# Inputs and result in the chip's own layouts; square root on ScalarE, its inverse on VectorE

## What is computed

```python
def layer_norm(x, g, b):
    mu = jnp.mean(xf, -1, keepdims=True)
    var = jnp.mean(jnp.square(xf - mu), -1, keepdims=True)
    return (xf - mu) * lax.rsqrt(var + LN_EPS) * g + b

def first_block(x, mem, ...):
    for i in range(DEPTH):                      # 2 layers
        h = diff_attention(x, ...) if i % 3 == 0 else dilated_attention(x, ...)
        x = layer_norm(ALPHA * x + h, ...)
        x = layer_norm(ALPHA * x + memory_cross_attention(x, mem, ...), ...)
        x = layer_norm(ALPHA * x + conv_glu(x, ...), ...)
    return x

def second_block(x, ...):
    proj = rms_norm_2(x, g_mix) @ w_in
    ...                                         # gated linear attention, sparse attention
    x = x + mixed @ w_out
    return x + hier_moe(rms_norm_2(x, g_ffn), ...)   # 32 experts
```

## Time and profile before

| | |
|---|---|
| median of 3 runs | 3189.44 us |
| lowest, highest | 3189.18, 3193.69 us |
| the profiled execution | 3190.67 us |
| its span, first to last instruction | 3188.9 us |
| TensorE: matmul, weight loads | 3019.6 us, 2417.7 us busy |
| VectorE, ScalarE, GpSimd | 1220.5, 1177.4, 1186.4 us busy |
| TensorE's mean granted clock | 0.96 |

### The profile page before, as it was taken

One profiled execution on the slowest core, in us unless ns is written; L12 is line 12 of the kernel. 1 busy time (PEld: TensorE's weight loads), 2 busy tenths in 40 slices (PEclk: granted clock), 3 DMA queues, 4 the chain that ended last, 5 costly groups with the idle time before them and its releaser, 6 DMA issues.

```text
span 3188.9 us, 38472 instructions
## 1 busy us (share of the span) xinstructions
PE 3019.6 (95%) x15009; PEld 2417.7 (76%) x15009; DVE 1220.5 (38%) x2249; ACT 1177.4 (37%) x1564; POOL 1186.4 (37%) x514
## 2 busy tenths in 40 slices
PE   8998998999989999998898999979989998999999
PEld 6765866888878888886866888858856876888887
DVE  2556327442432332335417443349143034232222
ACT  3565434322343343433434322363452234222222
POOL 3221523444433322231523444433232443444443
PEclk9999999999999999999999999988966999999999
DMA  4202412333342222211321333222211233343442
GB/s 136 67 27 67 132 53 66 94 104 93 108 124 80 67 72 75 67 54 61 124 67 53 104 94 92 85 64 70 76 35 48 77 101 89 117 119 99 122 112 83
DMA packets 366624, 269.30 MB, mean 84 GB/s; under 512 B 13328, under 2 KB 358851, under 8 KB 366476
## 3 DMA queue, kind: packets, MB, share of 16 engines
q1 hardware_dynamic: 366412, 267.14, 28.0%
q10 hardware_dynamic: 64, 0.10, 0.0%
HBM read 265.01 MB, written 6.39 MB: 85 GB/s over the span
## 4 chain that ended last, share of the span: by engine, by line
issue 46%; PE 35%; POOL 17%; ACT 1%; DVE 1%; POOLq 0%; DMA 0%; ACTq 0%; DVEq 0%; SPq 0%
POOL wl L592 11%; PE ps L1760 10%; PE ps L1761 10%; PE ps L1762 10%; POOL wl L590 6%; PE ps L2170 1%; PE ps L2187 1%; PE ps L1756 1%; PE ps L2091 0%; PE ps L2136 0%; PE ps L2159 0%; DVE X L1367 0%; POOLq L597 0%; PE ps L2074 0%; ACT X L826 0%
## 5 line engine op out<-in xcount | busy, mean ns | idle before, releaser
L590 POOL TENSOR_TENSOR wl<-raw,wh 128x1024 fp32r<-128x1024 f32 (+1 forms) x239 | 563.3, 2357 | 1902.8 <-ACT wh L632 1902.8
L1760 PE MATMUL ps<-xh,wh 128*128 128x512 f32 x2192 | 874.0, 399 | 48.5 <-issue 34.8
L1761 PE MATMUL ps<-xh,wl 128*128 128x512 f32 x2192 | 860.4, 392 | 0.0
L1762 PE MATMUL ps<-xl,wh 128*128 128x512 f32 x2192 | 859.7, 392 | 0.0
L632 ACT ACTIVATE wh<-raw 128x2048 fp32r<-128x2048 f32 (+1 forms) x239 | 450.6, 1886 | 901.6 <-PE ps L1762 859.2
L592 POOL TENSOR_TENSOR wl<-raw,wh 128x1024 fp32r<-128x1024 f32 (+1 forms) x239 | 605.8, 2535 | 0.0
L1760 PEld LDWEIGHTS ps<-xh,wh 128*128 128x128 f32 x2192 | 415.4, 190 | 164.3 <-issue 68.7
L1762 PEld LDWEIGHTS ps<-xl,wh 128*128 128x128 f32 x2192 | 415.4, 189 | 88.9
L1761 PEld LDWEIGHTS ps<-xh,wl 128*128 128x128 f32 x2192 | 415.9, 190 | 82.5
L1760 PE MATMUL ps<-ah,wh 128*128 128x512 f32 x864 | 340.0, 393 | 4.8 <-DVE X L1367 2.9
L1762 PE MATMUL ps<-al,wh 128*128 128x512 f32 x864 | 336.4, 389 | 0.0
(11 more groups left out here) (324 smaller groups left out, 3416.6 us busy)
## 6 DMA issues: line engine op xcount, KB each, us to landing
raw<-in_ffn_w_in SPq DMA_DIRECT2D x88, 512.0 KB, 5.0
raw<-in_dil_w_qkv SPq DMA_DIRECT2D x72, 512.0 KB, 4.6
raw<-in_w_in SPq DMA_DIRECT2D x42, 512.0 KB, 4.5
raw<-in_xatt_w_kv SPq DMA_DIRECT2D x32, 512.0 KB, 4.0
raw<-in_ffn_w_out SPq DMA_DIRECT2D x32, 512.0 KB, 4.1
raw<-in_w_gate SPq DMA_DIRECT2D x32, 512.0 KB, 5.0
raw<-in_w_up SPq DMA_DIRECT2D x32, 512.0 KB, 6.1
raw<-in_w_down SPq DMA_DIRECT2D x32, 512.0 KB, 4.5
```

What stands on the lines that cost most here:

```text
L590: pool.tensor_tensor(wl[:, s, 0:4, 0:n], raw[:, s, 0:4, 0:n], wh[:, s, 0:4, 0:n].bitcast(F32), ALU.subtract)
L1760: pe.matmul(dst, stat_h, mov_h, start=first, stop=False)
L1761: pe.matmul(dst, stat_l, mov_h, start=False, stop=False)
L1762: return pe.matmul(dst, stat_h, mov_l, start=False, stop=last)
```

## The change

- The host hands over `x` and `mem` already in the layout of `X`, and the parameters as the finished tile `par`; it turns the result back. So the transposes of x, of the parameters, of `mem` and of the result go, with their copies out of PSUM.
- SyncE loads unit 0, then x in four transfers, then unit 1, and the rest behind. ScalarE runs `high(0)` behind the second `xh`. The bias matmuls stand behind unit 2, and ScalarE's wait for the bias line's transfer stands at the fifth item of the attention.
- `mh` and `ml` are formed from the tile `memory_in` in SBUF, not from PSUM.
- The result leaves `X` directly, two chunks a transfer, each when its unit's additions are done.
- In the norms ScalarE takes a square root into `rstd`, and VectorE its reciprocal into bank `RSTD`. `roots()` loads ScalarE's table for the square root ahead of the units whose result a norm takes in (seven places in the program's run).

```diff
@@ sync
+            qkv = a["diff_w_qkv"][0]
+            square(Lin(0), qkv, 0)
+            for n in range(4):
+                sp.dma_start(X[:, 2 * n:2 * n + 2, :], a["x"][:, 2 * n:2 * n + 2, :]).then_inc(x_in[n], 16)
+            square(Lin(1), qkv, D)
             sp.dma_start(lamb[:, :, :].rearrange("p a b -> p (a b)"),
...
-            for role in range(2):
-                square(Lin(role), qkv, role * D)
...
+            sp.dma_start(par[:], a["params"]).then_inc(p_in, 16)
+            sp.dma_start(const[:], a["const"].rearrange("p (n m) -> p n m", m=P)).then_inc(const_in, 16)
...
-                sp.dma_start(mrows[:], a["mem"][0].rearrange("(t p) d -> p t d", p=P)).then_inc(m_in, 16)
+                sp.dma_start(memory_in[:], a["mem"]).then_inc(m_in, 16)
...
-            orows = out[0].rearrange("(t p) d -> p t d", p=P)
-            for q in range(4):
-                sp.wait_ge(o_cp, 2 * q + 2)
-                sp.dma_start(orows[:, :, q * UC:(q + 1) * UC], orow[:, :, q * UC:(q + 1) * UC]).then_inc(o_out, 16)
+            for k in range(4):
+                u = UNITS - 4 + k
+                sp.wait_ge(drained[u % 2], u // 2 * 2 + 2)
+                sp.dma_start(out[:, 2 * k:2 * k + 2, :], X[:, 2 * k:2 * k + 2, :]).then_inc(o_out, 16)
@@ scalar
+            def roots():
+                act.preload_act_table_set("sqrt_and_others")
+
+            for c in range(KC):
+                act.wait_ge(x_in[c // 2], 16)
+                act.activation(xh[:, c], X[:, c], ACT.Copy).then_inc(xh_ready, 1)
+                if c == 1:
+                    high(Lin(0))
+            high(Lin(1))
             act.wait_ge(lam_d, 4)
             act.activation(lam_e, lam_s, ACT.Exp).then_inc(lam_x, 1)
...
-            act.wait_ge(zs_out, 16)
+            def bias_line():
+                act.wait_ge(z_mm, 2)
+                for j in range(2):
+                    act.activation(zline[:, j * T:(j + 1) * T], ps[0:8, 5 + j], ACT.Copy).then_inc(z_cp, 1)
+                act.wait_ge(z_cp, 2)
+                act.dma_start(zscratch, zline[:]).then_inc(zs_out, 16)
...
+            bias_line()
             for n in range(DIFF_ITEMS + 6):
+                if n == TT:
+                    act.wait_ge(zs_out, 16)
                 diff_step(n)
...
                     act.wait_ge(ln_dve, 2 * n + 2)
-                    act.activation(rstd[:], acc_s[:, 0], ACT.Ln).then_inc(ln_act, 1)
+                    act.activation(rstd[:], acc_s[:, 0], ACT.Sqrt).then_inc(ln_act, 1)
...
-                    act.activation(rstd[:], ps[:, SQUARE], ACT.Ln, bias=eps_rms).then_inc(ln_act, 1)
-                act.wait_ge(ln_act, on_act - 1)
-                act.activation(ps[:, RSTD], rstd[:], ACT.Exp, scale=-0.5).then_inc(ln_act, 1)
+                    act.activation(rstd[:], ps[:, SQUARE], ACT.Sqrt, bias=eps_rms).then_inc(ln_act, 1)
...
             def memory(layer):
                 for b in range(4):
-                    act.wait_ge(mt_done, 4 * layer + b + 1)
-                    act.activation(mh[:, 2 * b:2 * b + 2, :], ps[:, 4 + b].rearrange("p (k t) -> p k t", k=2), ACT.Copy
+                    act.wait_ge(m_in, 16 * layer + 16)
+                    act.activation(mh[:, 2 * b:2 * b + 2, :], memory_in[:, 2 * b:2 * b + 2, :], ACT.Copy
                                    ).then_inc(mh_done, 1)
...
             def after_attention(layer):
+                roots()
...
+                roots()
                 residual(U_MO[layer], n0 + 1)
...
+                        roots()
                         residual(u0 + width, n0 + 2)
...
+            roots()
             residual(U_OUT, 7)
@@ vector
+            for c in range(KC):
+                dve.wait_ge(xh_ready, c + 1)
+                dve.tensor_tensor(xl[:, c], X[:, c], xh[:, c].bitcast(F32), ALU.subtract).then_inc(xl_ready, 1)
             dve.wait_ge(lam_in, 16)
...
                     for c in range(4):
                         centre(c)
                 dve.wait_ge(ln_act, on_act)
+                dve.reciprocal(ps[:, RSTD], rstd[:]).then_inc(inverse, 1)
+                own(inverse, n + 1)
...
-                    dve.tensor_tensor(ml[:, 2 * b:2 * b + 2, :], ps[:, 4 + b].rearrange("p (k t) -> p k t", k=2),
+                    dve.tensor_tensor(ml[:, 2 * b:2 * b + 2, :], memory_in[:, 2 * b:2 * b + 2, :],
                                       mh[:, 2 * b:2 * b + 2, :].bitcast(F32), ALU.subtract).then_inc(ml_done, 1)
@@ tensor
...
                 columns(Lin(0), xh, xl, ready=ready)
                 columns(Lin(1), xh, xl)
                 rows(Lin(2), xh, xl)
+                pe.wait_ge(z_in, 32)
+                for j in range(2):
+                    pe.matmul(ps[0:8, 5 + j, :], relb[:], hot[:, j * T:(j + 1) * T], start=True, stop=True
+                              ).then_inc(z_mm, 1)
+                pe.wait_ge(z_cp, 2)
+                pe.wait_ge(const_in, 16)
                 for n in range(DIFF_ITEMS + 4):
                     diff_step(n)
```

More of the change, by code:

```diff
@@ L270, in program @@
         drained = [sem("drained0"), sem("drained1")]
-        x_in, p_in, m_in, lam_in, z_in, zs_out = (sem(n) for n in ("x_in", "p_in", "m_in", "lam_in", "z_in", "zs_out"))
+        x_in = [sem(f"x_in{n}") for n in range(4)]
+        const_in, p_in, m_in, lam_in, z_in, zs_out = (
+            sem(n) for n in ("const_in", "p_in", "m_in", "lam_in", "z_in", "zs_out"))
         zc_out, mean_mm, keep_mm = sem("zc_out"), sem("mean_mm"), sem("keep_mm")
-        xt_done, par_t, par_s = sem("xt_done"), sem("par_t"), sem("par_s")
+        par_s = sem("par_s")
         z_mm, z_cp = sem("z_mm"), sem("z_cp")
@@ L279, in program @@
         stat_mm, ln_act, ln_dve = sem("stat_mm"), sem("ln_act"), sem("ln_dve")
-        cent, nrm, z_ready = sem("cent"), sem("nrm"), sem("z_ready")
+        cent, nrm, z_ready, inverse = sem("cent"), sem("nrm"), sem("z_ready"), sem("inverse")
         dbias_in = sem("dbias_in")
@@ L308, in program @@
         m_y, m_hh, m_hl = sem("m_y"), sem("m_hh"), sem("m_hl")
-        o_tr, o_cp, o_out = sem("o_tr"), sem("o_cp"), sem("o_out")
+        o_out = sem("o_out")
         f_cd, f_left, f_gd, f_hh, f_hl = (sem("f_" + n) for n in ("c", "left", "g", "hh", "hl"))
-        NORM_AT = [(n + 1, 3 * n + 3) for n in range(6)] + [(6, 20), (8, 22)]
+        NORM_AT = [(n + 1, 2 * n + 2) for n in range(6)] + [(6, 13), (8, 14)]
         MEAN, SQUARE, VAR, RSTD = 4, 5, 6, 7
@@ L650, in copy_out @@
                 copy_half(u, 1, dst, func, scale)
+            def roots():
[6 more added lines that the diff above has]
+            high(Lin(1))
             act.wait_ge(lam_d, 4)
             act.activation(lam_e, lam_s, ACT.Exp).then_inc(lam_x, 1)
[L655 to L663, removed]
-            act.activation(subln8, par[:, 0, R_SUBLN:R_SUBLN + 1], ACT.Copy, scale=1 - LAMBDA_INIT).then_inc(par_s, 1)
[L665 to L669, removed]
-            act.wait_ge(zs_out, 16)
+            act.wait_ge(p_in, 16)
+            act.activation(subln8, par[:, 0, R_SUBLN:R_SUBLN + 1], ACT.Copy, scale=1 - LAMBDA_INIT).then_inc(par_s, 1)
+            def bias_line():
[4 more added lines that the diff above has]
+                act.dma_start(zscratch, zline[:]).then_inc(zs_out, 16)
             def diff_store(u, role, j):
@@ L798, in norm @@
             def norm(n, g_row, b_row=None, keep=False, memory=None):
-                event, on_act = NORM_AT[n]
+                event, _ = NORM_AT[n]
                 if b_row is not None:
@@ L1190, in _ @@
                 over(act, u0 + PART_EXPERTS, 4, skip)
-            for c in range(KC):
-                act.wait_ge(o_tr, c + 1)
-                act.activation(orow[:, :, c * P:(c + 1) * P], ps[:, 4 + c % 4].rearrange("p (t n) -> p t n", t=TT),
-                               ACT.Copy).then_inc(o_cp, 1)
         @block.vector
@@ L1224, in _ @@
             dve.tensor_scalar(neglam, neglam, LAMBDA_INIT, None, ALU.subtract).then_inc(lam_d, 1)
-            for c in range(KC):
-                dve.wait_ge(xh_ready, c + 1)
-                dve.tensor_tensor(xl[:, c], ps[:, c % 4], xh[:, c].bitcast(F32), ALU.subtract).then_inc(xl_ready, 1)
             own(lam_d, 6)
@@ L1997, in after_attention @@
                 columns(Lin(u0 + 1), ah, al)
-                pe.wait_ge(m_in, 16 * (layer + 1))
-                for b in range(4):
-                    for k in range(2):
-                        for t in range(2):
-                            tr = flip(ps[:, 4 + b, k * M + t * P:k * M + (t + 1) * P],
-                                              mrows[:, t, (2 * b + k) * P:(2 * b + k + 1) * P])
-                    tr.then_inc(mt_done, 1)
                 columns(Lin(u0 + 2), ah, al)
@@ L2251, with by_chunk, parameters @@
         "w_out_2", "g_ffn_2", "w_rg_2", "b_rg_2", "w_re_2", "b_re_2", "w_gate_2", "w_up_2", "w_down_2"]
+def by_chunk(rows):
+    return np.ascontiguousarray(rows.reshape(rows.shape[0], KC, P).transpose(2, 1, 0))
+def parameters(inputs):
+    par = np.zeros((P, 3, P), np.float32)
```

(17 more changed lines are left out.)

58 lines of the change are left out of this document (6 added, 52 removed).

## The result

The changed kernel takes 3201.4 us in the median of six executions (3198.6 to 3206.1), against 3191.1 for the kernel before in six beside it. The ratio is 1.0033, with a 95% interval of 1.0020 to 1.0046. Measured again on another chip, both unchanged, it is 1.0033 (1.0022 to 1.0045). So it is slower, by about 10 us; the forecast of 3191 missed by that, though its range held the time. The profiled execution took 3198.6 us with a span of 3196.8, 7.9 more than before.

The account below looks back on a forecast made before the run. TensorE, busy 95% of the span, was taken as the bound. Terms -9.5 + 3.1 + 0.9 + 13.2 - 6.0 gave +1.7 us on the 3188.9 span, so 3191.0 us forecast, range 3177 to 3205.

Parts of the forecast that it names:

- The likeliest case: Whole kernel: time stays within the 0.2%, 6.4 us, that a measurement can tell; chance 0.53.
- the slow rival: Reciprocal takes 4.6 us on VectorE in all eight norms, TensorE waiting: total +12.9, 3202 us; chance 0.18.
- R: Time of one 128x512 reciprocal on VectorE in each norm; forecast 3.2 us, between ends of 0.69 and 4.6.
- The 178 ns row: Narrow reciprocal in the router, in the trace before; read as 8.7 ns an element, giving the 4.6 us upper end.
- The rule for norms 1, 2, 4 and 5: In these norms the first product starts R - 0.26 us later, the reciprocal standing behind four centrings.
- The sum of the norms: All eight norms together: 8R - 12.4, forecast as +13.2 us.
- R - 3.15: Claimed change in each of norms 0 and 3, where ScalarE's table load came late before, in us.
- The start: Before TensorE's first weight product: no transposes, quicker loads, start near 14.9 us; net -9.5 us.
- the late-start rival: At the start, GpSimd held or x late: TensorE starts at 18, total +5, 3195 us; chance 0.13.
- The bias matmuls: Placed behind unit 2, where TensorE does nothing else and waits for ScalarE's copies: +3.1 us.
- The memory step: Transposes of mem go, but splits are held by GpSimd: 0 in layer 0, +0.9 us in layer 1.
- The end: After the last addition to X: result transposes and copies go, most stores leave earlier; -6.0 us.

Follow-up runs that it names:

- the run with one table set: Changed kernel's layouts with Ln and Exp back on ScalarE, one table set holding both loaded early; 3174.3 us, ratio 0.9950 to the kernel before.

## Why the prediction was right and wrong

The frame held: two ends won, eight norms paid back, the rest at nothing. The likeliest case, no measurable difference, did not come. The time, 3201.4, is that of the slow rival (3202), but not by its mechanism: that wanted R = 4.6, and R was 3.36. So it was in part luck that the range held: its upper end stood at 3205 for a rival that did not happen, and other losses filled the gap.

**The reciprocal** was forecast at 3.2 us from narrow rows and is 3.36: 6.3 ns an element. The 178 ns row was the worse guide, and 4.6 too high. The Trainium skill, page "VectorE: DVE Perf Modes", section "First, the fixed hardware budget", with its repeat count of 8 gave an estimate of 4.4 us; the measurement says 3.36, so it does not hold here as I had turned it into time. The rule for norms 1, 2, 4 and 5, paid one for one, is shown at norm 1 by the table above and at all of them by the run with the reciprocal twice. The sum of the norms was forecast +13.2, and the ledger has 12.7 for them, 13.7 by the waits: R was 0.16 higher, which is +1.3, and norm 3 was 1.2 cheaper than R - 3.15, where a low-clock stretch is 3.4 us in place of 6.8; the 0.6 that is left is spread over the others.

**The start** failed in two terms, both small. `high(0)` ended at 10.97 and not 10.2, because x's first quarter was there at 8.03 and not 7.3, and GpSimd's two steps took 5.15 and not 4.66, beside VectorE's `xl` splits. That is the late-start rival in kind, at a third of its price: 16.21, where the forecast said 14.9 and the rival 18.

**The bias matmuls** cost 3.0 of 3.1 forecast, and moving them ahead of the first product showed that the place was all of the price, 3.1 at that point of the trace.

**The memory step** is where I misjudged a mechanism's size. I said that two splits would be held and that the wait behind them would cancel the 1.7 us of the transposes in layer 0 and cost 0.9 in layer 1. Held they were, 1.9 and 2.9 us for the first two and 5.9 for four, and TensorE did wait for X one unit later. But the wait in layer 1 was 2.63 us, more than the transposes had cost: +2.2 there and +0.4 in layer 0, together 1.7 above the forecast. From the last split to the end of the addition that frees the bank VectorE took 4.3 us in layer 1 (1516.3 to 1520.6) and 2.7 in layer 0: not only the addition but the scale steps too are slower there, and I had counted the addition alone. Of the 2.2, 0.8 is the low-clock stretch behind the wait: the run with one table set had the same wait and no such stretch, and took 48.61 us in place of 49.40.

**The end** gave -6.6 for -6.0: the last store landed in 2.6, quicker than any of the four in the burst before.

**What the sum left out** is TensorE's clock. I priced it at the start, and excluded it at the norms, rightly: the low clock behind norm 1 covers the same 11 or 12 products in both kernels, and grows over the longer rest alone. But two more low-clock stretches, near 1642 and 2710, cost 3.6 us in places that the change does not touch. That is over half of the 6.2 us between the forecast span and the measured one; the rest is the start (+1.1), the memory step (+1.7) and drifts (+1.0), less 0.6 at the end and 0.5 at the norms. Another 3.9 us of the ten are the profiled executions' places among the others: I took the kernel before's to be 1.2 above its median, and the changed kernel's lay 2.7 below its own.

## What to carry over

Before moving a function to VectorE to save a table load on ScalarE, ask what the load costs where it stands: here it was hidden in four norms of eight, the replacement cost 3.36 us in each, and naming a table set that holds both functions saved the load for nothing and won 22 us with the layouts and the start. A step behind which TensorE stands still is paid in full, so one row of its true duration is worth more than every other term; where no such row exists, the forecast should rest most of its width on it. For a change of many small shifts a range should leave room for low-clock stretches that arise elsewhere; here they were 3.6 us.

## What was not expected of the hardware

A reciprocal of 128x512 in fp32 takes 3.35 to 3.36 us on VectorE in all eight norms, five times a multiplication's 0.68. GpSimd's 2.35 us step became 3.40 when VectorE's step with two operands in SBUF had begun 0.05 us before it, and VectorE's 0.69 us steps became up to 2.9 when GpSimd was first. TensorE's low stretches, at its 1.2 GHz level, began at the same places within 1 us in two executions of the changed kernel on two chips, all but the first (222 and 225 us).
